# A diffusion backbone in two layers: every h tile and every weight slot in SBUF lengthened by 16 unused bytes

## Chip, cores and metric

One Trainium2 chip, one of its cores. The metric is the device time of one execution in microseconds (us), the median of the runs shown; lower is better. A nanosecond (ns) is a thousandth of that.

## What is computed

The reference is a two-layer backbone over 512 latent tokens and 256 context tokens, width 1024, in float32. Each layer is: a half-step SwiGLU block, a token mixer, another half-step SwiGLU block, each between two RMS norms with scale, shift and gate from a conditioning vector. The mixer of layer 0 is windowed attention beside bidirectional retention, that of layer 1 a gated long convolution.

```
def swiglu(h, w_gate, w_up, w_down):
    return (jax.nn.silu(h @ w_gate) * (h @ w_up)) @ w_down

for l in range(DEPTH):                      # 2 layers
    x = macaron_half(x, ...)                # swiglu, D=1024, D_FF=2816
    ctx = macaron_half(ctx, ...)            # layer 0 alone
    h = adaln_in(x, ...)
    y = even_mixer(h, hc, ...) or hyena_mixer(h, ...)
    x = adaln_out(x, y, ...)
    x = macaron_half(x, ...)
```

## The kernel before, in words

Activations lie transposed: 128 channels on the partitions, tokens along the free dimension. `x`, `h_hi` and `h_lo` are eight tiles of 512 float32 values (2048 bytes) per partition each. Weights come in blocks of 128 output columns: `raw`, `w_hi` and `w_lo` are rings of four slots of 1024 values (4096 bytes), and in a slot stand up to eight pieces of 128x128 weights, 512 bytes apart.

Nearly float32 products come from three fast matmuls in the format float32r. A value is split into a rounded part (hi, written by ScalarE) and the rest (lo, written by VectorE), and the helper `three` (lines 495 to 499) adds hi x hi, hi x lo and lo x hi in PSUM:

```
pe.matmul(out, w_hi[:, slot, c:c + P], hi, start=start, stop=False)
pe.matmul(out, w_hi[:, slot, c:c + P], lo, start=False, stop=False)
return pe.matmul(out, w_lo[:, slot, c:c + P], hi, start=False, stop=stop)
```

The first operand is the stationary one: 128 columns of weights, loaded by an instruction of their own (PEld in the profile) while the matmul before runs. The second is streamed past them: 512 token columns, or 256 for the context.

Per block of weights the flow is: SP's queue brings the block into `raw`; ScalarE writes `w_hi` (line 1027) once the block that used the slot four blocks ago is multiplied; VectorE writes `w_lo` = `raw` - `w_hi` (line 1466); TensorE runs 24 matmuls (8 tiles times three), or 15 to 18 in the down projections. There are 442 blocks. Each SwiGLU block is two rounds of gate and up (h tiles times weights, 24 and 20 blocks) and down (the tiles `act_hi`, `act_lo` times weights, 16 blocks each); the SwiGLU blocks on the context use 256 columns. The input and output projections of both mixers multiply `h_hi`/`h_lo` too, for the context `hc_hi`/`hc_lo`. Attention, retention, the filters and the convolution use plain float32 matmuls, which the records show as two passes each (lines 567, 965, 975, 978 among them). The order of the work is written out by hand, with semaphores; it is the same in both kernels.

Where a tensor lies follows from the order of the allocations: the first begins at byte 16,512 of each partition, each later one behind the one before, rounded up to 32 bytes. A tensor allocated in a scope of its own (`with ExitStack() as r`) gives its room back at once, so that what is allocated next lies over it: `filt` and `term` lie over `h_hi` and `h_lo`, `spare_hi` over `w_hi`, `spare_lo` over `w_lo`. Each is used only while the other is not. First bytes, and what they leave over modulo 64:

```
tensor        before            after
h_hi          16,512  (0)       16,512  (0)
h_lo          32,896  (0)       33,024  (0)
w_hi          82,048  (0)       82,304  (0)
w_lo          98,432  (0)       98,752  (0)
act_hi       158,624 (32)      158,528  (0)
act_lo       183,200 (32)      183,104  (0)
hc_hi        179,104 (32)      179,008  (0)
hc_lo        187,296 (32)      187,200  (0)
taps0        142,240 (32)      142,144  (0)
dft_f        203,680 (32)      203,584  (0)
u            166,816 (32)      166,720  (0)
dft          187,840  (0)      187,744 (32)
```

Before the change all tiles, slots and pieces of weights are multiples of 512 bytes apart, so every tile of a tensor has the remainder of its first.

Of the kernel before, what the change touches and what calls it, by code (L numbers as in the profile page):

```python
# [18 lines left out]
F32R = mybir.dt.float32r  # L19
# [4 lines left out]
P = 128  # L24
D = 1024
KT = D // P
SEQ = 512
# [9 lines left out]
QK_SCALE = HEAD ** -0.5  # L37
RING = 4
BANKS = 4
IN_TILES = 22  # L40
MASK_W = 3 * P
G_LOW = -2 * P
# [100 lines left out]
def build(nc, io):  # L143
    stages = []

    def stage(name, src, blocks, cols, mods=None):
        s = Stage(src, blocks, cols, mods)
        s.first = stages[-1][1].first + stages[-1][1].blocks if stages else 0
        stages.append((name, s))
        return s  # L150
# [8 lines left out]
    for s in (ffns[0][3], ffns[1][0], ffns[1][3]):  # L159
        s.unrolled = True  # L160
    mix_in = stage("mix_in", io["mix_in"], IN_TILES, 1024)
    mix_out = stage("mix_out", io["mix_out"], KT, 1024)
# [19 lines left out]
    with ExitStack() as ctx:  # L182
        def sb(name, shape, dt=F32):
            return ctx.enter_context(nc.sbuf_tensor(name, shape, dt))
# [12 lines left out]
            c_wide = r.enter_context(nc.sbuf_tensor("c_wide", [P, KT, 32], F32))  # L197

        with ExitStack() as r:
            h_hi = r.enter_context(nc.sbuf_tensor("h_hi", [P, KT, SEQ], F32R))  # L200
            h_lo = r.enter_context(nc.sbuf_tensor("h_lo", [P, KT, SEQ], F32R))

        filt = sb("filt", [P, 3, 4, 512])
        term = sb("term", [P, 2, 1024])
        x = sb("x", [P, KT, SEQ])
        raw = sb("raw", [P, RING, 1024])
        with ExitStack() as r:
            w_hi = r.enter_context(nc.sbuf_tensor("w_hi", [P, RING, 1024], F32R))
        spare_hi = sb("spare_hi", [P, RING, 1024])
        with ExitStack() as r:  # L210
            w_lo = r.enter_context(nc.sbuf_tensor("w_lo", [P, RING, 1024], F32R))
        spare_lo = sb("spare_lo", [P, RING, 1024])
        idle_hi, idle_lo = (v[:, 0:2, :].rearrange("p b c -> p (b c)") for v in (spare_hi, spare_lo))
        mod = sb("mod", [P, 2, NMOD, 2, KT])
# [5 lines left out]
        c_cols = sb("c_cols", [P, KT, 2])  # L220
        c_silu = sb("c_silu", [P, KT, 2])
        ident = sb("ident", [P, P])
        ones = sb("ones", [P, P])
        eps = sb("eps", [P, 1])
        prod = sb("prod", [P, 2, SEQ])
        square = sb("square", [P, 2, SEQ])
# [260 lines left out]
        def _(pe):  # L487
# [132 lines left out]
            def down(s, T, tiles, beside=lambda i: None):  # L620
# [4 lines left out]
                def step(i, last):  # L625
                    for dd in range(2):
                        bank = DOWN_BANK[dd]
                        if dd or not isinstance(i, int) or i:

                            pe.wait_ge(result_read, BANKS + p0 + 2 * i + dd - 1)  # L630
                        for half in range(2):
# [201 lines left out]
            def attention_retention():  # L833
# [3 lines left out]
                pe.wait_ge(v_ready, len(VALUES))  # L837
                pe.wait_ge(result_read, at["p"] + BANKS)

# [96 lines left out]
            def hyena():  # L936
# [22 lines left out]
                def forward(c, units):  # L959
                    for m in units:  # L960
                        n = 8 * c + m
                        if n >= 4:
                            pe.wait_ge(uf_ready, n - 3)
                        for k in range(2):
                            ins = pe.matmul(psum[:, 4 + n % 4, :], dft[:, k, m % 4, :],
                                            u[:, 2 * (m // 4) + k, c * 512:c * 512 + 512], start=(k == 0), stop=(k == 1))
                        ins.then_inc(uf_sum, 1)
# [34 lines left out]
                forward(1, range(8))  # L1002
                pe.wait_ge(result_read, at["p"] + BANKS)
                for i, part in CONV_PARTS:
# [13 lines left out]
        def _(act):  # L1018
# [3 lines left out]
            def split_hi(b0, i, cols):  # L1022

                slot = b0 % RING
                act.wait_ge(raw_landed[slot], 16 * (i + b0 // RING + 1))
                act.wait_ge(block_done, b0 + 4 * i + 1)
                act.activation(w_hi[:, slot, 0:cols], raw[:, slot, 0:cols], ACT.Copy).then_inc(hi_split, 1)  # L1027
# [18 lines left out]
            def gate_up(s, T, beside=lambda i, j: None):  # L1046
                b0, p0, f0 = s.first, at["p"], at["f"]

                def step(i, last):
                    for j in range(2):  # L1050
# [7 lines left out]
                        act.activation(silu[:, j, 0:T], psum[:, bank, 0:T], ACT.Silu).then_inc(silu_ready, 1)  # L1058
                        act.wait_ge(result_read, BANKS + p0 + 4 * i + 2 * j + 2)
                        act.activation(act_hi[:, bass.ds(2 * i + j, 1), 0:T], prod[:, j:j + 1, 0:T],  # L1060
# [30 lines left out]
            def down(s, T, final, beside=lambda i, j: None, gain=None):  # L1091
                n0, p0 = KT * at["norm"], at["p"]

                def step(i, last):
                    for dd in range(2):
# [6 lines left out]
                        if final:  # L1102
                            act.wait_ge(result_read, BANKS + p0 + 2 * i + dd + 1)
                            act.wait_ge(square_used, n0 + 2 * i + dd - 1)
# [129 lines left out]
            def mixer_in():  # L1234
# [55 lines left out]
                act.wait_ge(gate_ready, 1)  # L1290
                act.wait_ge(block_done, RING + mix_in.first + IN_TILES)
                act.activation(silu_g, rg[:], ACT.Silu).then_inc(gate_ready, 1)
# [78 lines left out]
            def project(s, gain):  # L1371
                n0, p0 = KT * at["norm"], at["p"]
                warm_root()
                for d in range(KT):
                    split_ahead(s.first + d)
                    if d == KT - 1:
                        split_hi(s.following.first + 2, 0, 1024)
                    act.wait_ge(result_read, BANKS + p0 + d + 1)
                    act.wait_ge(square_used, n0 + d - 1)
# [1051 lines left out]
```

## Time and profile before

| | |
|---|---|
| median of 3 runs | 2561.92 us (2561.21 to 2564.89) |
| profiled execution | 2561.9 us, the time from its first to its last instruction |
| TensorE matmuls (PE) | 2434.9 us busy, 95% |
| TensorE weight loads (PEld) | 1957.6 us, 76% |
| VectorE (DVE) | 1416.1 us, 55% |
| ScalarE (ACT) | 888.9 us, 35% |
| GpSimd (POOL) | 127.5 us, 5% |
| mean granted TensorE clock | 0.971 |

The busy time of matmuls is the union of their records. One record runs from the start of a matmul to the end of its last result, so neighbours overlap, and the mean duration of one is longer than the distance to the next. That distance can be read where the timeline lists single starts, or from the length of a stretch and the number of matmuls in it.

### The profile page before, as it was taken

The numbers are of one execution on the slowest core, as the hardware profiler recorded it, in microseconds if no ns is written. First come the engines' busy times: TensorE is split into PE (matmuls) and PEld (weight loads), VectorE is DVE, ScalarE is ACT, GpSimd is POOL, SyncE is SP. The second block draws the span as 40 slices with busy tenths as digits, with TensorE's granted clock in tenths as the row PEclk, the third lists the DMA queues.
The fourth block names the chain that finished last, engine by engine and source line by source line (L and its number), as shares of the span: only waits on it lengthen the run. The fifth ranks groups of instructions, "written<-read, shape, count | busy, mean of one in ns | idle before, by whom it ended". The sixth has DMA issues, their size and how long they took to land. (4 is left out here: it accounts for less than half of the span.)

```text
span 2561.9 us, 31755 instructions
## 1 busy us (share of the span) xinstructions
PE 2434.9 (95%) x11758; PEld 1957.6 (76%) x11758; DVE 1416.1 (55%) x1969; ACT 888.9 (35%) x1296; POOL 127.5 (5%) x216
## 2 busy tenths in 40 slices
PE   6999999999899888899999999999999998999997
PEld 2688888899778544778888778888878677888886
DVE  5767833565653578653257663563575397532334
ACT  1532133444531375542222342222344313422221
POOL 1011100000000111000001000010000000000000
PEclk8999999999999999989999989999989998999999
DMA  8577832455422100222357422462222213223322
GB/s 322 218 274 258 304 102 71 136 163 192 143 65 74 56 1 1 73 97 90 99 180 254 160 67 98 166 245 92 89 85 99 85 62 99 67 89 107 99 74 74
DMA packets 94976, 322.11 MB, mean 126 GB/s; under 512 B 11408, under 2 KB 11824, under 8 KB 93072
## 3 DMA queue, kind: packets, MB, share of 16 engines
q1 hardware_dynamic: 67824, 221.75, 25.5%
q0 software_dynamic: 26032, 97.60, 11.3%
q8 instruction: 73, 1.20, 0.2%
q10 hardware_dynamic: 1008, 1.25, 0.1%
q14 instruction: 39, 0.32, 0.0%
HBM read 312.16 MB, written 8.39 MB: 125 GB/s over the span
## 5 line engine op out<-in xcount | busy, mean ns | idle before, releaser
L497 PE MATMUL psum<-h_hi,w_hi 128*128 128x512 f32 (+1 forms) x2256 | 855.8, 379 | 28.7 <-DVE h_lo L1684 13.3
L498 PE MATMUL psum<-h_lo,w_hi 128*128 128x512 f32 (+1 forms) x2256 | 846.4, 375 | 0.0
L499 PE MATMUL psum<-h_hi,w_lo 128*128 128x512 f32 (+1 forms) x2256 | 846.4, 375 | 0.0
L1466 DVE TENSOR_TENSOR w_lo<-raw,w_hi 128x1024 fp32r<-128x1024 f32 (+2 forms) x442 | 470.4, 1099 | 95.3 <-ACT w_hi L1027 92.1
L497 PEld LDWEIGHTS psum<-h_hi,w_hi 128*128 128x128 f32 x2256 | 429.2, 190 | 113.1 <-issue 28.7
L1027 ACT ACTIVATE w_hi<-raw 128x1024 fp32r<-128x1024 f32 (+2 forms) x442 | 406.2, 951 | 270.3 <-PE psum L499 223.1
L499 PEld LDWEIGHTS psum<-h_hi,w_lo 128*128 128x128 f32 x2256 | 428.7, 190 | 76.4
L498 PEld LDWEIGHTS psum<-h_lo,w_hi 128*128 128x128 f32 x2256 | 429.4, 190 | 75.1 <-issue 1.7
L497 PE MATMUL psum<-act_hi,w_hi 128*128 128x512 f32 (+1 forms) x880 | 331.0, 376 | 9.2 <-issue 5.2
L498 PE MATMUL psum<-act_lo,w_hi 128*128 128x512 f32 (+1 forms) x880 | 329.6, 374 | 0.0
L499 PE MATMUL psum<-act_hi,w_lo 128*128 128x512 f32 (+1 forms) x880 | 329.5, 374 | 0.0
L1600 DVE TENSOR_TENSOR prod<-psum,square 128x512 f32<-128x512 f32 (+1 forms) x110 | 70.1, 637 | 443.2 <-PE psum L499 431.1
L1060 ACT ACTIVATE act_hi<-prod 128x512 f32 (+3 forms) x110 | 64.8, 589 | 504.7 <-DVE prod L1600 504.7
L497 PEld LDWEIGHTS psum<-act_hi,w_hi 128*128 128x128 f32 x880 | 166.7, 189 | 42.3 <-issue 10.3
L499 PEld LDWEIGHTS psum<-act_hi,w_lo 128*128 128x128 f32 x880 | 166.8, 189 | 32.7
L498 PEld LDWEIGHTS psum<-act_lo,w_hi 128*128 128x128 f32 x880 | 166.7, 189 | 32.0
L1501 DVE SCALAR_TENSOR_TENSOR mod_acc<-mod_raw,c_silu,mod_acc 128x1024 f32<-128x1024 f32 x133 | 170.7, 1283 | 10.5 <-DMA mod_raw<-in_w_mod 3.4
L2240 POOL DMA_DIRECT2D mod_raw<-in_w_mod x168 | 89.1, 530 | 934.9 <-DVE mod_acc L1498 536.5
L1058 ACT ACTIVATE square<-psum 128x512 f32<-128x512 f32 (+1 forms) x110 | 60.6, 551 | 204.7 <-PE psum L499 204.6
L1605 DVE TENSOR_TENSOR act_lo<-prod,act_hi 128x512 f32 (+3 forms) x110 | 70.3, 639 | 91.1 <-ACT act_hi L1060 91.1
L1705 DVE COPY y<-psum 128x512 f32<-128x512 f32 (+3 forms) x40 | 25.5, 638 | 123.9 <-PE psum L499 123.8
L1105 ACT ACTIVATE square<-y 128x512 f32<-128x512 f32 (+2 forms) x40 | 23.5, 588 | 153.8 <-DVE y L1707 153.8
(279 smaller groups left out, 1915.5 us busy)
## 6 DMA issues: line engine op xcount, KB each, us to landing
raw<-in_gate_up SPq DMA_DIRECT2D x220, 512.0 KB, 4.2
mod_raw<-in_w_mod POOLq DMA_DIRECT2D x168, 512.0 KB, 5.3
raw<-in_down_a SPq DMA_DIRECT2D x80, 384.0 KB, 3.8
raw<-in_down_b SPq DMA_DIRECT2D x80, 320.0 KB, 3.1
raw<-in_hy_in SPq DMA_DIRECT2D x24, 512.0 KB, 3.4
raw<-in_mix_in SPq DMA_DIRECT2D x22, 512.0 KB, 3.5
filt_dram<-made SPq DMA_DIRECT2D x6, 1024.0 KB, 4.2
taper<-in_decay SPq DMA_DIRECT2D x8, 512.0 KB, 9.3
```

Source lines behind the costliest of these rows:

```text
L497: pe.matmul(out, w_hi[:, slot, c:c + P], hi, start=start, stop=False)
L498: pe.matmul(out, w_hi[:, slot, c:c + P], lo, start=False, stop=False)
L499: return pe.matmul(out, w_lo[:, slot, c:c + P], hi, start=False, stop=stop)
L1027: act.activation(w_hi[:, slot, 0:cols], raw[:, slot, 0:cols], ACT.Copy).then_inc(hi_split, 1)
L1058: act.activation(silu[:, j, 0:T], psum[:, bank, 0:T], ACT.Silu).then_inc(silu_ready, 1)
L1060: act.activation(act_hi[:, bass.ds(2 * i + j, 1), 0:T], prod[:, j:j + 1, 0:T], ACT.Copy).then_inc(act_hi_ready, 1)
L1466: ins = dve.tensor_tensor(w_lo[:, slot, 0:cols], raw[:, slot, 0:cols], w_hi[:, slot, 0:cols].bitcast(F32), ALU.subtract)
L1501: ins = dve.scalar_tensor_tensor(mod_acc[:, :], src, c, mod_acc[:, :], ALU.mult, ALU.add)
L1600: ins = dve.tensor_tensor(prod[:, j, 0:T], psum[:, bank, 0:T], silu[:, j, 0:T], ALU.mult)
L1605: dve.tensor_tensor(act_lo[:, fl, 0:T], prod[:, j:j + 1, 0:T], act_hi[:, fl, 0:T].bitcast(F32), ALU.subtract).then_inc(act_ready, 1)
L1705: dve.tensor_copy(dst, src).then_inc(result_read, 1)
L2240: pool.dma_start(mod_raw[:, k % RING, :], io["w_mod"][layer, v, k]).then_inc(mod_landed[k % RING], 16)
```

## The change

Each of the eight tiles of `h_hi` and `h_lo` and each of the four slots of `w_hi` and `w_lo` gets four more float32 values (16 bytes) that nothing reads or writes. `h_hi` and `h_lo` are now views of the first 512 values of each row; the weight rings are only indexed up to 1024. So tile k begins at first byte + 2064k instead of + 2048k, slot s at + 4112s instead of + 4096s. Three small allocations (`h_pad`, `w_hi_pad`, `w_lo_pad`) keep the tensors that lie over them long enough. `ones`, of which only the first column is ever read, shrinks from 128 columns to one. Together these move what is allocated after `ones` by 96 bytes down (`prod`, `square`, `full`, `act_hi`, `act_lo`, `hc_hi` and the rest). `raw`, `act_hi`, `act_lo`, `hc_hi` and `hc_lo` keep their tile lengths. No instruction is added, removed or moved on any engine.

```
+TILE_PAD = 4
...
-            h_hi = r.enter_context(nc.sbuf_tensor("h_hi", [P, KT, SEQ], F32R))
-            h_lo = r.enter_context(nc.sbuf_tensor("h_lo", [P, KT, SEQ], F32R))
+            h_hi_rows = r.enter_context(nc.sbuf_tensor("h_hi", [P, KT, SEQ + TILE_PAD], F32R))
+            h_lo_rows = r.enter_context(nc.sbuf_tensor("h_lo", [P, KT, SEQ + TILE_PAD], F32R))
+            h_hi, h_lo = h_hi_rows[:, :, 0:SEQ], h_lo_rows[:, :, 0:SEQ]
 
         filt = sb("filt", [P, 3, 4, 512])
+        sb("h_pad", [P, 2 * KT * TILE_PAD])
         term = sb("term", [P, 2, 1024])
         x = sb("x", [P, KT, SEQ])
         raw = sb("raw", [P, RING, 1024])
         with ExitStack() as r:
-            w_hi = r.enter_context(nc.sbuf_tensor("w_hi", [P, RING, 1024], F32R))
+            w_hi = r.enter_context(nc.sbuf_tensor("w_hi", [P, RING, 1024 + TILE_PAD], F32R))
+        sb("w_hi_pad", [P, RING * TILE_PAD])
         spare_hi = sb("spare_hi", [P, RING, 1024])
         with ExitStack() as r:
-            w_lo = r.enter_context(nc.sbuf_tensor("w_lo", [P, RING, 1024], F32R))
+            w_lo = r.enter_context(nc.sbuf_tensor("w_lo", [P, RING, 1024 + TILE_PAD], F32R))
+        sb("w_lo_pad", [P, RING * TILE_PAD])
         spare_lo = sb("spare_lo", [P, RING, 1024])
...
-        ones = sb("ones", [P, P])
+        ones = sb("ones", [P, 1])
```

## Rows read from the trace of the kernel before

**Rows 1.** The page's first part: busy us (share of the span) x instructions.
```profile
span 2561.9 us, 31755 instructions
...
PE 2434.9 (95%) x11758; PEld 1957.6 (76%) x11758; DVE 1416.1 (55%) x1969; ACT 888.9 (35%) x1296; POOL 127.5 (5%) x216
```

**Rows 2.** Grouped lines by shape, TensorE: names, shapes xcount | busy us, mean ns.
```profile
L497 PE MATMUL psum<-h_hi,w_hi 128*128 128x512 f32 x1904 | 754.5, 396 | 24.3 <-DVE h_lo L1684 13.3 <-issue 4.4 <-DVE prod L1990 3.8
...
L497 PE MATMUL psum<-act_hi,w_hi 128*128 128x512 f32 x704 | 280.5, 399 | 0.0
...
L497 PE MATMUL psum<-h_hi,w_hi 128*128 128x256 f32 x352 | 101.3, 288 | 4.4 <-DVE w_lo L1466 4.4
...
L497 PE MATMUL psum<-act_hi,w_hi 128*128 128x256 f32 x176 | 50.5, 287 | 9.2 <-issue 5.2 <-DVE w_lo L1466 4.1
...
L497 PE MATMUL psum<-hc_hi,w_hi 128*128 128x256 f32 x80 | 22.3, 279 | 0.0
```

**Rows 3.** Windows: h x512, act x512, h x256, act x256; the head names the columns.
```profile
core 0: us, PE busy (x) PEld busy (x) DVE busy (x) ACT busy (x) POOL busy (x), PEclk, DMA share, GB/s
2379.36:2488.19 108.83, 108.83 (x481) 90.09 (x480) 35.79 (x39) 29.18 (x38) 0.00 (x0) 1.00 0.27 86
2488.19:2544.19 56.00, 56.00 (x241) 44.98 (x240) 22.05 (x31) 15.34 (x24) 0.00 (x0) 1.00 0.19 59
593.25:650.84 57.59, 57.59 (x482) 57.59 (x481) 30.78 (x39) 25.85 (x39) 0.00 (x0) 1.00 0.55 173
567.96:593.24 25.28, 25.28 (x219) 25.28 (x218) 13.94 (x18) 10.81 (x12) 0.00 (x0) 1.00 0.61 204
```

**Rows 4.** Timeline of TensorE, h tiles at 512 columns: start us, duration us.
```profile
324.08 0.39 PE L497 MATMUL psum<-h_hi,w_hi 128*128 128x512 f32 x1
324.30 0.39 PE L498 MATMUL psum<-h_lo,w_hi 128*128 128x512 f32 x1
324.53 0.39 PE L499 MATMUL psum<-h_hi,w_lo 128*128 128x512 f32 x1
324.76 0.39 PE L497 MATMUL psum<-h_hi,w_hi 128*128 128x512 f32 x1
```

**Rows 5.** Timeline of TensorE, act tiles at 512 columns.
```profile
422.72 0.39 PE L497 MATMUL psum<-act_hi,w_hi 128*128 128x512 f32 x1
422.95 0.40 PE L498 MATMUL psum<-act_lo,w_hi 128*128 128x512 f32 x1
423.19 0.39 PE L499 MATMUL psum<-act_hi,w_lo 128*128 128x512 f32 x1
423.42 0.40 PE L497 MATMUL psum<-act_hi,w_hi 128*128 128x512 f32 x1
```

**Rows 6.** Timeline of TensorE, hc tiles at 256 columns, first and last of four.
```profile
755.59 0.28 PE L497 MATMUL psum<-hc_hi,w_hi 128*128 128x256 f32 x1
...
755.94 0.28 PE L497 MATMUL psum<-hc_hi,w_hi 128*128 128x256 f32 x1
```

**Rows 7.** Timeline of TensorE, float32 passes back to back, and the duration of one.
```profile
84.81 3.60 PE L567 MATMUL psum<-taps,dft_f 128*128 128x512 f32 x8
...
2036.73 9.60 PE L965 MATMUL psum<-u,dft 128*128 128x512 f32 x22
...
L567 PE MATMUL psum<-taps,dft_f x96: 592/592/1190, 45.5 to 94.2; 128*128 128x512 f32 x96
```

**Rows 8.** Timeline of the start.
```profile
0.97 0.17 DVE L1456 MEMSET ones<- 128x128 f32 x1 [0.97 <-PEq L2422]
...
5.14 2.05 PE L541 MATMUL psum<-pos,hid_w 128*128 128x512 f32 x2 [5.14 <-DMA fb<-in_hy_fb]
```

**Rows 9.** Grouped lines by shape, ScalarE and VectorE: mean ns after the busy us.
```profile
L1144 ACT ACTIVATE full<-prod,mod,gain_in 128x512 f32<-128x512 f32 x48 | 39.1, 814 | 49.3 <-DVE prod L1673 41.2 <-DVE prod L1750 8.1
...
L1425 ACT ACTIVATE short<-zp,hy_cols 128x512 f32<-128x512 f32 x16 | 13.1, 818 | 3.4 <-DVE u_t L2192 2.9
...
L1425 ACT ACTIVATE x<-zp,hy_cols 128x512 f32<-128x512 f32 x8 | 6.5, 815 | 0.3
...
L1664 DVE SCALAR_TENSOR_TENSOR x<-square,gain_out,x 128x512 f32<-128x512 f32 x32 | 23.8, 742 | 0.0
...
L2189 DVE SCALAR_TENSOR_TENSOR short<-zp,hy_cols,short 128x512 f32<-128x512 f32 x16 | 12.0, 752 | 0.6
...
L1817 DVE SCALAR_TENSOR_TENSOR x<-y,gain_out,x 128x512 f32<-128x512 f32 x8 | 6.0, 752 | 0.3
```

## Prediction

> **What bounds the kernel now.** The page's first part [rows 1] gives TensorE 2434.9 us of matmul in a span of 2561.9 us; the next engine, VectorE, has 1416.1 us. The grouped lines [rows 2] say which matmuls these are: the three of the helper `three`, lines 497 to 499, 128x512 and 128x256 in shape. The counts are three lines each: 3 x 1904 = 5712 at 512 columns from the h tiles, 3 x 704 = 2112 at 512 columns from the act tiles, 3 x 352 = 1056, 3 x 176 = 528 and 3 x 80 = 240 at 256 columns from h, act and hc. Their "mean ns of one" is a latency and overlaps its neighbours, so the cost of one more or one less is not there. It is the spacing of starts, and that is read from stretches in which TensorE does nothing else and never waits [rows 3]: each has busy time equal to its length, the granted clock at 1.00 (the 2.4 GHz level) and VectorE and ScalarE busy for less than 0.55 of it. So in these stretches the time is the number of matmuls times their spacing, and nothing else.
>
> The spacing, from the start times in the timeline and the counts (the TensorE count in [rows 3] holds one to three more that were already running at a window's edge or fall in the last nanoseconds; the length belongs to 480, 240, 480 and 216 of them):
> - h tiles, 512 columns: 108.83 us / 480 = 226.7 ns. The starts [rows 4] show it step by step: 324.08, 324.30, 324.53, 324.76.
> - act tiles, 512 columns: 56.00 / 240 = 233.3 ns; the starts step by 0.23 to 0.24 us [rows 5].
> - h tiles, 256 columns: 57.59 / 480 = 120.0 ns.
> - act tiles, 256 columns: 25.28 / 216 = 117.0 ns; hc tiles start 0.12 apart, 755.59 to 755.94 in three steps, 117 ns [rows 6].
>
> Same instruction, weights from the same ring, same number of columns, and yet 512 columns take 6.6 ns longer from act and 256 columns 3.0 ns less. What differs is where the operands lie. By the address table h and the weights have the same low address (difference 0 modulo 64 bytes), act and hc stand 32 bytes off. The columns themselves are 106.7 ns per 256 at 2.4 GHz (226.7 - 120.0, from two rows, is exactly that). So above the bare columns a matmul pays 13.3 ns with difference 0 at either length, 20.0 ns (512) or 10.3 ns (256) with difference 32. That the addresses matter at all is thus in the trace. It is not in plain float32 passes: with difference 0 (line 567, eight in 3.60 us, (3.60 - 0.59) / 7 = 430 ns) and with difference 32 (line 965, 22 in 9.60 us, (9.60 - 0.59) / 21 = 429 ns) they are spaced alike [rows 7]. They take two cycles a column, 426.7 ns, and so pay about 3 ns for a new set of weights. That is the least overhead that any row shows.
>
> **The change, part by part.** No instruction is added, taken away or moved. One gets smaller: the memset of `ones`, 0.17 us for 128 columns [rows 8]. It ends at 1.14 us, and the first matmul starts at 5.14 us behind a DMA: worth nothing, and if the cover were gone 0.1 us.
>
> *The low addresses.* In the changed kernel h tile k starts 16k bytes further in modulo 64, weight slot s 16s bytes, and act and hc tiles start at 0 modulo 64 instead of 32. The difference h minus weights is 16(k - s), so over eight k and four slots it is 0, 16, 32 and 48 in equal parts; for act and hc it is -16s, again equal parts. The sum therefore needs the spacing at four differences. Two are measured. No row shows a fast matmul at 16 or 48. Their bounds: at best such a tile pays only the 3.3 ns of [rows 7], 213.3 + 3.3 = 216.6 ns (110.0 at 256 columns). At worst it goes above the dearest known one by the step between the two known ones, 233.3 + 6.6 = 240 ns (120 at 256); that is a bound by extension, since no row lies higher. I take the middle of the two known values, 230.0 and 118.5 ns, because the unknown differences lie between the known ones and the known rows are far nearer to each other than to either bound. Then all matmuls go to 230.0 and 118.5:
> - 5712 from h at 512: (230.0 - 226.7) x 5712 = +18.8 us
> - 2112 from act at 512: (230.0 - 233.3) x 2112 = -7.0 us
> - 1056 from h at 256: -1.5 x 1056 = -1.5 us
> - 768 from act and hc at 256: +1.5 x 768 = +1.1 us
>
> Sum +11.4 us, all on the path, since TensorE never waits in these stretches. 2561.9 + 11.4 = 2573.3 us; the profiled span of 2561.9 equals the median of the runs, so I forecast 2573. With the lower bound for the odd differences all matmuls average 223.3 and 114.3 ns: -19.5 - 21.2 - 6.0 - 2.2 = -48.9 us, 2513. With the upper one 235.0 and 119.3: +47.3 + 3.5 - 0.8 + 1.7 = +51.7, 2614. The point from which the sign turns is 227.0 ns for the odd differences: they must be as good as the best that is known. Every nanosecond there is 7824 / 2 = 3.9 us.
>
> The Trainium skill speaks against any effect: "TensorE: Matmul & The Clock Gate", in the section "Step-by-step: what each phase is for", has two independent SBUF read ports, one for the streamed operand and one for the weights, so that a weight load takes nothing from a running matmul. By that rule the change is worth 0 and the time stays 2562. The trace disagrees in part: 226.7 against 233.3 ns is a difference that the rule does not allow, unless something other than the low address makes it.
>
> *The other engines.* ScalarE and VectorE write and read the moved tiles. The trace has odd addresses already: the rows of `zp` start 4 bytes in and are 2056 bytes apart. ScalarE reads them in 0.815 to 0.818 us, and aligned tiles in the same kind of instruction in 0.814; VectorE takes 0.752 us for a three-operand instruction there and 0.742 to 0.752 for aligned ones [rows 9]. So splits, h tiles and act tiles cost what they did. Were each of the 442 splits of weights 10 ns longer, it would stay off the path: weights arrive ahead, and VectorE is idle half of the time [rows 3]. The DMAs write the same 4096-byte rows to `raw`.
>
> **Rivals.**
> 1. *The odd differences are the good ones.* If two read streams meet in the same part of the memory when they are 0 or 32 apart and miss each other at 16 and 48, these pay 3 ns. For it: of the 13.3 ns per matmul at difference 0, 10 are unexplained, since the float32 passes take new weights for 3. Against it: going from 0 to 32 bought nothing at 512 columns. Price: down to 2513; at 222 ns (114 at 256 columns), 2538.
> 2. *They are the dear ones*: a stream that begins 16 bytes into a wider unit needs one more read. 240 ns, 2614. For it: 32 costs more than 0 at 512 columns; against: at 256 it costs less.
> 3. *The low address is not the cause.* act and hc also lie far up, above byte 158,000, with h and the weights below 115,000. If the part of the memory makes the difference, padding does nothing: 2562. Nothing in the trace separates the two. The rule of the Trainium skill named above leads to the same time.
> 4. *Only the streamed operand's own low address counts.* Then act goes wholly to the values of 0: -6.6 x 2112 = -13.9, and +3.0 x 768 = +2.3; h still spreads, +18.8 - 1.5. Sum +5.7, 2568.
>
> **How the numbers follow.** The middle case 0.32, rival 2 0.08, rival 4 0.05, all slower: 0.45. Rival 3 with the narrow band around 227 ns in which gain and loss cancel: 0.22. Rival 1 in any strength: 0.33. A measurement of this kernel tells about 0.2%, 5 us, from no change. The likeliest case's own range is 2567 to 2590. The range over all of them drops the far ends of rivals 1 and 2, about a tenth each: 2530 (220.5 ns at the odd differences, 112 at 256 columns) to 2606 (238 and 119.5).
>
> **What would show it.** In the profile after, the same stretches of one kind should again have TensorE busy throughout, and the count decides: per step of four slots the spacing should no longer be constant but change with tile and slot. Right: starts of 227 where k equals s modulo 4, 233 where they are two apart, and about 230 between; the act stretch of 240 matmuls in about 55.2 us and the h stretch of 480 in 110.4. Wrong: odd pairs at 217 to 222 ns (rival 1), at 240 (rival 2), or every h start still 226.7 and every act start still 233.3 apart (rival 3), or act wholly at 226.7 (rival 4). Idle time of TensorE should stay near 127 us, and line 1027 and line 1466 should keep their means; if they do not, the part on the other engines is wrong.

## The result, and the profile after

The changed kernel takes 2586.17 us (median of 4 runs, 2581.98 to 2587.38), the kernel before 2563.24 us in the same set. The ratio is 1.008 with a 95% interval of 1.0067 to 1.0092: 0.8% slower, some 23 us. The forecast was 2573 us, slower, in a range of 2530 to 2606.

The page of the changed kernel, first part, against [rows 1]:

```profile
span 2585.6 us, 31755 instructions
...
PE 2458.2 (95%) x11758; PEld 1960.8 (76%) x11758; DVE 1416.6 (55%) x1969; ACT 889.6 (34%) x1296; POOL 127.4 (5%) x216
```

The span grew by 23.7 us and the matmuls' busy time by 23.3; TensorE's idle time is 127.4 us where it was 127.0. So nothing waits longer. VectorE and ScalarE moved by 0.5 and 0.7 us. The splits of the weights keep their means, though they now write at 0, 16, 32 and 48 modulo 64 (`w_lo` took 1220 ns before, `w_hi` 1047):

```profile
L1471 DVE TENSOR_TENSOR w_lo<-raw,w_hi 128x1024 fp32r<-128x1024 f32 x282 | 335.4, 1221 | 76.0 <-ACT w_hi L1032 73.6
L1032 ACT ACTIVATE w_hi<-raw 128x1024 fp32r<-128x1024 f32 x282 | 286.3, 1049 | 95.1 <-PE psum L504 60.3 <-DMA raw<-in_gate_up 18.8 <-DMA raw<-in_hy_out 10.8
```

The windows of the same four kinds of stretch (length, TensorE busy, count, granted clock, DMA), against [rows 3]:

```profile
2400.24:2511.61 111.37, 111.37 (x481) 1.00 0.26 84
2511.61:2567.16 55.55, 55.55 (x242) 1.00 0.19 60
598.88:655.59 56.71, 56.71 (x483) 1.00 0.54 174
573.25:598.88 25.63, 25.63 (x220) 1.00 0.62 201
```

Divided by the same 480, 240, 480 and 216 matmuls, the spacing of starts is 232.0 ns for h at 512 columns (it was 226.7), 231.5 for act at 512 (233.3), 118.1 for h at 256 (120.0), 118.7 for act at 256 (117.0). With the counts of the prediction: +5.3 x 5712 = +30.3 us, -1.9 x 2112 = -4.0, -1.9 x 1056 = -2.0, +1.7 x 768 = +1.3. That is +25.6 us for a measured 23.7 of span, so the spacing accounts for all of it. The sum overshoots by 1.9 us, more than rounding gives. In the two profiled executions the granted clock also differs a little outside the dense stretches (mean 0.971 before, 0.973 after), and the sum does not count that.

Where h had one step before (226 or 227 ns, save a handful), it now has many. The timeline of TensorE at one of the worst places, a block of weights in slot 1 at tile 4:

```profile
2419.39 0.40 PE L504 MATMUL psum<-h_hi,w_lo 128*128 128x512 f32 x1
2419.62 0.42 PE L502 MATMUL psum<-h_hi,w_hi 128*128 128x512 f32 x1
2419.88 0.41 PE L503 MATMUL psum<-h_lo,w_hi 128*128 128x512 f32 x1
2420.12 0.40 PE L504 MATMUL psum<-h_hi,w_lo 128*128 128x512 f32 x1
2420.36 0.39 PE L502 MATMUL psum<-h_hi,w_hi 128*128 128x512 f32 x1
```

The steps are 0.23, 0.26, 0.24 and 0.24 us; the 0.26 is well above anything in [rows 4] or [rows 5]. No wait ends there, and the pattern comes back with slot and tile. By the single starts in the trace of this last h stretch, the three matmuls of tile 4 in slot 1 average 245.0 ns over the five blocks that use that slot, those of tile 6 in slot 3 average 242.7 and those of tile 2 in slot 2 238.9; no other pair of slot and tile is above 235. So the placement decides. But it does not decide by tile number minus slot number (k - s in the prediction) alone: that is 3 for tile 4 in slot 1 and for tile 6 in slot 3, and also for tile 3 in slot 0 and tile 5 in slot 2, which average 232.5 and 232.1.

### The profile page after: what moved, and what is told of

The parts are those of the page before. It is cut to its first block and busy times, and to the rows that moved or that the text cites. A ratio compares the mean times of both kernels' runs of the same rounds, so it can differ in the third digit from the quotient of the medians.

```text
span 2585.6 us, 31755 instructions
## 1 busy us (share of the span) xinstructions
PE 2458.2 (95%) x11758; PEld 1960.8 (76%) x11758; DVE 1416.6 (55%) x1969; ACT 889.6 (34%) x1296; POOL 127.4 (5%) x216
## 5 line engine op out<-in xcount | busy, mean ns | idle before, releaser
L1710 DVE COPY y<-psum 128x512 f32<-128x512 f32 (+3 forms) x40 | 25.5, 638 | 118.1 <-PE psum L504 117.9
```

Of the source, the lines that this page charges most:

```text
L1710: dve.tensor_copy(dst, src).then_inc(result_read, 1)
```

## The experiments

Below, "difference" is the first byte of the streamed tile minus that of the weights, within the pair hi and hi and the pair lo and lo. The windows named hold the same 480 matmuls from h and 240 from act as before, near the end of the program, unless said otherwise.

### First set: is it the low address, and what of it

In these four kernels every tensor that the fast matmuls read gets 64 spare bytes and starts at a chosen place in them; tile and slot strides are 2048 and 4096 bytes again, so no tile differs from its neighbour. `ones` has one column, as in the change. At shift 0 the tensors are all at 0 modulo 64.

```
+        def shifted(make, name, n, cols, at, dt):
+            rows = make(name, [P, n * cols + ROOM], dt)
+            return rows[:, at:at + n * cols].rearrange("p (n c) -> p n c", c=cols)
...
+            h_hi = shifted(own, "h_hi", KT, SEQ, H_AT, F32R)
+            h_lo = shifted(own, "h_lo", KT, SEQ, H_LO_AT, F32R)
...
+            w_hi = shifted(own, "w_hi", RING, 1024, W_AT, F32R)
+        spare_hi = shifted(sb, "spare_hi", RING, 1024, W_AT, F32)
```

**all0**: all shifts 0.

> All fast operands at 0 modulo 64: h and w as before (though no longer alike modulo 512), act and hc moved by 32 bytes to 0. If the low address modulo 64 governs (difference or own address alike), h tiles stay at 226.7 ns (512 columns) and 120.0 (256), act falls from 233.3 to 226.7 ns at 512 and rises from 117.0 to 120.0 at 256: -6.6 x 2112 + 3.0 x 768 = -11.6 us, about 2551 us, faster than both kernels. If the part of the memory governs (high address), nothing changes: 2563. If more address bits than six matter, h leaves 226.7.

Measured 2594.39 us against 2564.23, ratio 1.0106 (1.0085 to 1.0127). Slower than the kernel before, not faster, and no better than the changed one. Windows, h and act at 512 columns:

```profile
2410.32:2521.77 111.45, 111.45 (x481) 1.00 0.27 84
2521.77:2577.76 55.99, 55.99 (x241) 1.00 0.19 59
```

h is at 232.2 ns though its difference modulo 64 is 0, as it was before. The spare bytes had made the full difference -128 modulo 256: before, h and weights were alike in more bits than six. The modulus of the prediction falls here.

**swap_h32**: h shifted by 32.

> h tiles moved as a whole to 32 modulo 64, weights at 0, act and hc at 0: the two streams have changed places. If the low address governs, h takes act's values, 233.3 ns at 512 and 117.0 at 256, and act takes h's: +6.6 x 5712 - 3.0 x 1056 - 13.9 + 2.3 = +22.9 us, about 2586. If the part of the memory governs: 2563, h still 226.7, act still 233.3.

Measured 2605.58 us (one run), against 2586 expected. h 112.00 us / 480 = 233.3, act 56.00 / 240 = 233.3. h has the value expected at 512 columns, act does not return to 226.7; its difference is -64.

**both32**: h and weights shifted by 32.

> h and weights both at 32, act and hc at 0. If the difference modulo 64 governs, h is at 226.7 and 120.0 and act at 233.3 and 117.0 (as in the kernel before, 2563). If the streamed operand's own address governs, h is at 233.3 and 117.0 and act at 226.7 and 120.0, as in the run with h alone at 32 (2586).

Measured 2595.02 us (one run). Windows:

```profile
2406.88:2518.33 111.45, 111.45 (x481) 1.00 0.26 84
2518.33:2574.33 56.00, 56.00 (x242) 1.00 0.19 59
```

Neither expectation came true. h moved by 32 bytes together with its weights takes 111.45 us, the figure of all0, and not the 112.00 of h in swap_h32, which has the same own address. That points to the difference and not to the own address, but by half a microsecond only: 232.2 against 233.3 ns. The second set separates the two more clearly.

**odd16**: h shifted by 16, act and hc by 48.

> h at 16, act and hc at 48, weights at 0; no tile differs from its neighbour. If the sum of the prediction was only mis-sized, the odd differences cost about 234 ns each at 512 columns (from the means of the changed kernel: 4 x 232.05 - 226.7 - 233.3 = 2 x 234.0 for h): h +7.3 x 5712 = +42 us, act about 0, 2605 or so. If the odd values are as good as the middle that was forecast, 230 ns: h +19, act -7, 2575. If what costs in the changed kernel is that neighbouring tiles differ, the odd values may be as low as 227 and the time near 2560.

Measured 2583.5 us (one run), which is none of the three times: h 110.95 / 480 = 231.1 at difference -112, act 55.49 / 240 = 231.2 at -16. An odd multiple of 16 is no dearer than an even one.

### Second set: the modulus, and a better placement

Here h, weights and act keep their form and are pushed by gaps: one between `term` and `x` (before the weights), one before `act_hi` and one before `hc_hi`.

```
         term = sb("term", [P, 2, 1024])
+        sb("gap", [P, GAP])
         x = sb("x", [P, KT, SEQ])
...
-        ones = sb("ones", [P, P])
+        ones = sb("ones", [P, 1])
...
+            rb("act_gap", [P, ACT_GAP])
             act_hi = rb("act_hi", [P, 12, SEQ], F32R)
...
+                rb("hc_gap", [P, ACT_GAP])
                 hc_hi = rb("hc_hi", [P, KT, CTX], F32R)
```

**alike512**: no gap before the weights, 192 bytes before act and before hc. Everything that the fast matmuls read then starts at 128 modulo 512.

> h and weights exactly where they were in the kernel before; act and hc moved so that they too have the weights' address modulo 512 (all at 128). Theory A, the difference between the streamed tile and the weights modulo 512 bytes sets the spacing and 0 is its best value: act falls from 233.3 to 226.7 ns at 512 columns (-6.6 x 2112 = -13.9 us) and act and hc rise to 120.0 at 256 (+2.3): 2564 - 11.6 = about 2552 us. Theory B, only the h and weight tensors among themselves count (or the address modulo 2048): act stays at 233 and the time at 2564.

Measured 2551.43 us (2548.62 to 2555.53, 6 runs) against 2565.02: ratio 0.9955 (0.9941 to 0.9969). Faster than both: by 0.45% than the kernel before, by some 35 us than the changed one. Windows of h at 512, act at 512, h at 256, act at 256:

```profile
2368.23:2477.03 108.80, 108.80 (x482) 1.00 0.27 86
2477.03:2531.43 54.40, 54.40 (x242) 1.00 0.19 61
592.45:650.05 57.60, 57.60 (x483) 1.00 0.54 172
566.46:592.45 25.99, 25.99 (x220) 1.00 0.59 200
```

act takes 54.40 us for 240, 226.7 ns, and 25.99 for 216, 120.3 ns. Both are h's figures, though act still lies above byte 158,000. That ends the rival that the part of the memory matters (rival 3), and the expectation came true to within a microsecond. The single starts here also answer whether the other engines' traffic makes the spacing. The 480 steps of h are all 226 or 227 ns, and their mean is 226.6 ns both where VectorE or ScalarE works nearly all through the step and where both are idle. The same holds for act in the kernel before, at 233.4 ns either way.

**h256_act64**: gap 256, act gap 256. Differences 256 for h and 64 for act.

> No tile differs from its neighbour; difference (streamed minus weights, modulo 512) 256 for h, 64 for act and hc. If the good place is 0 modulo 256, h stays at 226.7 ns and the time near 2564; if it is 0 modulo 512 alone, h goes to 231 to 233 ns, +25 to +38 us, 2590 to 2600. act at 64: 230 to 233.5 like the other differences measured so far.

Measured 2548.02 us (one run). Windows:

```profile
2364.20:2473.05 108.85, 108.85 (x482) 1.00 0.27 86
2473.05:2528.00 54.95, 54.95 (x242) 1.00 0.19 60
```

h is still at 226.8 ns: the good place is 0 modulo 256. act at 64 gives 229.0, below the range that was expected. One run of 2548.0, just under the spread of alike512 (2548.6 to 2555.5), does not rank this kernel against it.

**hm192_act160**: gap 192, act gap 352. Differences -192, which is 64 modulo 256, and 160.

> Difference -192 for h, 160 for act. Theory A: h at 231 to 233.5 ns, +25 to +38 us, act 231 to 233.5: 2585 to 2602. A value below 226.7 at either would be a better place than the one the kernel before has.

Measured 2575.86 us (one run), below the range expected. Windows, h and act at 512:

```profile
2389.11:2498.99 109.88, 109.88 (x482) 1.00 0.27 85
2498.99:2555.22 56.23, 56.23 (x241) 1.00 0.19 59
```

h is at 228.9 ns, act at 234.3. The range for h is missed on the good side: -192 is 64 modulo 256, and 228.9 is the value that act had at 64 in h256_act64 (229.0), as a period of 256 bytes asks.

**h128_actm32**: gap 384, act gap 160. Differences 128 and -32.

> Difference +128 for h, -32 for act. Theory A: h at 231 to 233.5 ns, act at 231 to 233.5, about 2585 to 2602. If -32 and +32 bytes lie close enough to 0 to keep its value, act is at 227 to 229.

Measured 2595.42 us (one run). Windows, h and act at 512:

```profile
2407.55:2519.10 111.55, 111.55 (x481) 1.00 0.26 84
2519.10:2575.10 56.00, 56.00 (x241) 1.00 0.19 59
```

h is at 232.4 ns, act at 233.3, as expected; 32 bytes off on either side of 0 costs the same 6.6 ns. These last kernels separate difference from own address. h lies at the same bytes in all of them and in the kernel before, 16,512 and 32,896, and only the weights (with what is allocated behind them) have moved: 108.83 us before, 108.85 at 256, 109.88 at -192, 111.55 at 128. In alike512 the weights kept their bytes and act moved, from 233.3 to 226.7 ns. Neither address alone does it.

### Third set: the two halves of the change, and what meets what

**pad_h_only**: the 16 bytes on the h tiles as in the change, none on the weight slots. act and hc are placed at difference 0.

> The 16 bytes on the h tiles alone; weights, act and hc have one address modulo 256 (difference 0 for act). Theory A, now with the modulus 256 (256 for h gave 226.8 ns, 64 gave 229.0 in two kernels): h runs through 16k and, in the h_lo matmuls, -128 + 16k, and averages near 231 ns, act stays at 226.7: 2551 + 4.3 x 5712 = about 2576 us. If what costs is the step from one tile to the next, h comes out above every value of a uniform kernel, over 234.

Measured 2577.95 us (10 runs) against 2565.37, ratio 1.0043 (1.003 to 1.0055). Windows, h and act at 512:

```profile
2392.47:2503.75 111.28, 111.28 (x481) 1.00 0.26 84
2503.75:2558.15 54.40, 54.40 (x241) 1.00 0.19 61
```

h at 231.8 ns, act at 226.7 as if nothing had been done to it. Starts at line 502, one per tile, in one block show the tile at work (0.69 us is 230 ns a matmul, 0.71 is 237):

```profile
2420.25 0.39 PE L502 MATMUL psum<-h_hi,w_hi 128*128 128x512 f32 x1
...
2420.94 0.39 PE L502 MATMUL psum<-h_hi,w_hi 128*128 128x512 f32 x1
...
2421.63 0.39 PE L502 MATMUL psum<-h_hi,w_hi 128*128 128x512 f32 x1
...
2424.41 0.40 PE L502 MATMUL psum<-h_hi,w_hi 128*128 128x512 f32 x1
...
2425.12 0.39 PE L502 MATMUL psum<-h_hi,w_hi 128*128 128x512 f32 x1
```

Tiles 0 and 1 take 0.69 us each, tile 6 takes 0.71. Over all blocks of the stretch the starts give 228.8 ns a matmul for tile 0 and 235.2 for tile 6, which is above every uniform placement, though the mean of all tiles is not. Against alike512, which differs in the pads alone, this half costs 26.5 us.

**pad_w_only**: the 16 bytes on the weight slots alone.

> The 16 bytes on the weight slots alone; h and act at one address modulo 256. The difference is -16s for the hi weights and -64 - 16s for the lo weights (the hi ring's pad pushes the lo ring by 64). From the uniform kernels (0: 226.7, -16: 231.2, -32: 233.3, -64: 233.3, -96: 233.3, -112: 231.2 ns) both h and act average about 231.4: 2551 + 4.7 x 7824 = about 2588 us. Within one block of weights the spacing should be steady, and change from slot to slot.

Measured 2585.74 us (4 runs), ratio to the kernel before 1.0066 (1.004 to 1.0091). Windows, h and act at 512:

```profile
2400.05:2511.37 111.32, 111.32 (x481) 1.00 0.26 84
2511.37:2567.05 55.68, 55.68 (x241) 1.00 0.19 60
```

h is at 231.9 ns, act at 232.0. The weights' pad hits h and act alike and costs 34 us over alike512. The two halves do not add: 26.5 and 34 us each by itself, 35 us together. h averages 231.8 with the pad on the tiles, 231.9 with it on the slots and 232.0 with both. By the starts, the mean changes from slot to slot as expected (230.9, 233.2, 232.2 and 231.4 ns for slots 0 to 3 in the last h stretch), but within a block of weights the spacing is not steady: in one block the eight tiles took between 0.69 and 0.71 us.

**h16_actm48**: the shifts of the first set with a gap of 128 bytes before `x`; h and act shifted by 16. Differences 16 and -48.

> Two differences not yet measured, both odd multiples of 16 and the same for all tiles: 16 for h, -48 for act. Theory A: 230 to 234 ns each, 2580 to 2600 us; at -16 it was 231.2. If there is a place better than 0, it must be one of the few left, and would read below 226.7.

Measured 2582.11 us (one run). h 110.92 / 480 = 231.1 ns in its last stretch, act 56.00 / 240 = 233.3. But h has two levels in this one execution. Two windows of 480 matmuls each, the second from a later block of the same kind:

```profile
1526.13:1636.02 109.89, 109.89 (x481) 1.00 0.29 95
2210.02:2320.95 110.93, 110.93 (x481) 1.00 0.29 90
```

That is 228.9 against 231.1 ns, with the same code and the same addresses.

**pairs**: `h_lo` and `w_lo` moved by 160 bytes together, the rest at one address modulo 256.

```
+            r.enter_context(nc.sbuf_tensor("lo_gap", [P, 40], F32))
             h_lo = r.enter_context(nc.sbuf_tensor("h_lo", [P, KT, SEQ], F32R))
...
+        sb("w_gap", [P, 24])
         with ExitStack() as r:
             w_hi = r.enter_context(nc.sbuf_tensor("w_hi", [P, RING, 1024], F32R))
...
+        sb("w_lo_gap", [P, 40])
         with ExitStack() as r:
             w_lo = r.enter_context(nc.sbuf_tensor("w_lo", [P, RING, 1024], F32R))
```

> h_lo and w_lo moved by 160 bytes together; h_hi, w_hi, act_hi, act_lo left at one address modulo 256. Theory C, what meets is the streamed tile and the weights that are being loaded for the next matmul: h_hi meets w_hi, h_lo meets w_lo (difference 0 in all three), so h stays at 226.7 ns; act_lo meets w_lo at -160, so for act the matmul of line 498 is the slow one, act above 227 ns. Theory D, what meets is the streamed tile and its own weights: h_lo x w_hi at 160 and h_hi x w_lo at -160 are slow, h averages about 231 ns, and for act line 499 is the slow one. Time: C about 2555, D about 2580.

Measured 2592.3 us (one run). Windows, h and act at 512:

```profile
2404.69:2515.98 111.29, 111.29 (x482) 1.00 0.26 84
2515.98:2571.97 55.99, 55.99 (x241) 1.00 0.19 59
```

Neither time came true, 2555 or 2580. Theory C falls: h is at 231.9 ns, not 226.7, although every tile stands at difference 0 to the weights loaded beside it. Theory D has the mean of h about right. Its act fails: line 499 (505 here) was to be the slow matmul. By the starts it is the middle one in four of the six long stretches (236.0 ns in the one from 428 us, against 230.9 and 233.0), as C had it, yet the other two are slow as well. In the last stretch, the one shown, it is not even that: the three lines take 234.5, 233.9 and 231.6 ns, for the same mean of 233.3. So which of the three is slow is no property of the addresses, and single lines cannot decide between such theories. In these runs only kernels with all four of a product's tensors at one address modulo 256 had the best value, and neither simple pairing explains the rest.

All uniform placements together, with the difference modulo 256, in ns per matmul, from one execution each and from the windows near the end (512 columns) and near 600 us (256 columns):

```
difference  512 columns   256 columns   from
0           226.7         120.0-120.3   before h, alike512, h256_act64 h
16          231.1 (229.0) 116.7         h16_actm48 h *
32          233.3         117.0         before act
64          228.9, 229.0  117.8, 118.2  hm192_act160 h, h256_act64 act
128         232.2, 232.4  118.7-119.7   all0 h *, both32 h *, h128_actm32 h
144         231.1         117.7         odd16 h *
160         233.3, 234.3  117.8-119.1   swap_h32 h *, both32 act *, hm192_act160 act
192         233.3         118.9         all0 act *, swap_h32 act *
208         233.3         118.1         h16_actm48 act *
224         233.3         118.7         h128_actm32 act
240         231.2         118.2         odd16 act *
* lo tensors 64 bytes further modulo 256 than hi tensors, in weights and tiles alike
```

Steps of 1 or 2 ns between rows above 228 mean little. By the starts, h16_actm48 is not the only kernel with two levels: h of h128_actm32 runs at 232.4 ns in most stretches and at 233.3 in others, act of odd16 at 231.1 and in three short stretches at 233.2, act of h16_actm48 at 233.3 and once at 231.2.

## Why the prediction was right, and where it was off

**The bound.** Right: TensorE never waits in the dense stretches, and the change of their spacing times the counts gives the change of the span (25.6 against 23.7 us). Idle time stayed at 127 us. A detail of the reading is off: in the act stretch of 256 columns VectorE is busy for 0.551 of the time, not less than 0.55.

**The other engines.** Right: lines 1027 and 1466 of before kept their means, and the memset brought nothing visible. The reading from `zp` is loose for VectorE, whose line 2189 starts 8 bytes into a row and not 4.

**The sign.** Right, for the reason given in outline: h and the weights left a good relative address, act left a bad one, and there are 5712 of the one and 2112 of the other. Part of it is luck. The forecast gave "slower" 0.45, and the sign hung on 230.0 ns for differences that no row showed, with the turning point at 227.0. The two errors of the sum, modulus and middle value, both made the change look cheaper than it is, so neither could turn the sign.

**The size.** Off by a factor of two: +11.4 forecast, +22.9 measured by the medians. The step that failed is "the difference h minus weights is 0, 16, 32 and 48 in equal parts", modulo 64 bytes. The measured modulus is 256 (h256_act64 against all0 and h128_actm32). The first bytes in the address table, taken modulo 256, already part the tensors: before the change h and weights are all at 128, after it `h_lo` is at 0 and `w_lo` at 192. With six bits the sum let a quarter of the h matmuls keep 226.7 ns, and a quarter of the act matmuls reach it. In truth h runs over differences from -48 to 112 and, in the lo pair, from 16 to 176, because the pads of `h_hi` push `h_lo` by 128 bytes more against `h_hi`, and those of the hi ring push the lo ring by 64; none of them meets all its tensors at 0. Nor is the spacing a function of that difference alone, which the sum took for granted: 232.5, 245.0, 232.1 and 242.7 ns in slots 0 to 3 where k - s is 3. The term of h at 512 columns was sized +18.8 and is +30.3; that of act was -7.0 and is -4.0; those at 256 columns were -1.5 and +1.1 and are -2.0 and +1.3. The middle value of 230.0 ns for the unknown differences was a fair guess for 16 and 64 (229 to 231) and too low for most others (231 to 234).

**The rivals.** Rival 1, that the odd differences are the good ones: no; 16, 144, 208 and 240 gave 231 to 233 ns, and no placement tried had a mean below 226.7. Rival 2, 240 ns: single steps in the last h stretch of the changed kernel reach 255 ns, but no uniform placement has a mean above 234.3. Rival 3, the part of the memory: refuted by alike512. Rival 4, the streamed operand's own address: refuted by hm192_act160 and h128_actm32, where h kept its bytes and took 109.88 and 111.55 us instead of 108.83. The rule of the Trainium skill, in "TensorE: Matmul & The Clock Gate", "Step-by-step: what each phase is for", that weight loads take nothing from a running matmul, would have left the time at 2562 us. The traces do not agree with it for these float32r matmuls, as far as the spacing depends on where the weights lie: 480 of them take 108.83 to 111.55 us with h at the same bytes. That it is the weight load that costs the time is argued from this, not shown.

**The signs to look for.** Starts of 227 ns where k equals s modulo 4 did not show (those pairs average 229.1 to 238.9 ns in the last h stretch), which is the same failure of the modulus. Means of 230.0 were expected in both stretches; 232.0 and 231.5 came.

## What to carry to other kernels

Look at the distance between starts of matmuls, not at their duration, and compare it between operands: the same instruction at two distances means that something about the operands costs time. For float32r matmuls of 512 columns here, put the streamed tiles and the weights, hi and lo, at one address modulo 256 bytes; tiles of 2048 bytes and slots of 4096 keep that by themselves, and a pad meant to spread them destroys it. At 256 columns the same place is the dearest, by some 3 ns, so count which of the two shapes there is more of. A tensor that is small and read only in part (`ones`) may be all the room one needs: alike512 is 192 bytes of gap and 0.45% faster.

## What the runs showed of the hardware that was not expected

- Where all tiles and slots stand alike, the mean spacing of float32r matmuls goes with the difference between the first bytes of streamed tile and weights, with a period of 256 bytes: 226.7 ns at 0, 229 at 64, 229 or 231 at 16, 231 to 234 at the others measured, for 512 columns. The period rests on h at 256 (226.8 ns) and on -192 and 64 (228.9 and 229.0).
- At 256 columns the order is another: 0 is the dearest (120.0 to 120.3 ns) and 16 and 32 the cheapest (116.7 and 117.0).
- At difference 16 the same code with the same addresses ran steadily at 229 ns in some stretches and at 231.1 in others, and two other kernels have such levels. So the address is not all: something that a stretch begins with is kept through it. Which of the three lines of `three` is the slow one is kept in the same way: at difference 64 (h of hm192_act160) the lines take 231.7, 225.8 and 229.3 ns in one stretch and 225.9, 229.2 and 231.6 in another, for one mean of 228.9. The 234.3 beside 233.3 at 160 is likewise unexplained.
- What in the memory or in TensorE makes the difference, and which reads meet, stays open. The run on pairs speaks against the two simple readings and puts nothing in their place.
